# Moving operand of the 512-column weight products: stored reversed by the host, streamed with step minus one

## The reference

```python
proj = rmsnorm(x) @ w_in                  # 2048 -> 6144
x = x + mixed @ w_out                     # 2048 -> 2048
x = x + relu(rmsnorm(x) @ w_up)**2 @ w_down
proj2 = rmsnorm(x) @ w_in_2               # 2048 -> 7168
x = x + mixed2 @ w_out_2
y = (gate * gelu(xn @ u.T)) @ v           # 16384 experts
```

## Time and profile before

| what | value |
|---|---|
| device time, three runs | 3211.2 us median (3210.97 to 3211.51) |
| span of the profiled execution, first to last instruction | 3209.0 us |
| device time of the profiled execution itself | not listed; the median lies 2.2 us above the span |
| PE busy | 3191.6 us, 99% |
| PE weight loads (overlapping PE) | 2854.0 us, 89% |
| DVE, ACT, POOL busy | 2030.1, 1447.3, 496.9 us |
| DMA | 644 MB, 201 GB/s on average |
| matmul records | 19,975 |

### The profile page before, as it was taken

One profiled execution on the slowest core, in us unless ns is written; L12 is line 12 of the kernel. 1 busy time (PEld: TensorE's weight loads), 2 busy tenths in 40 slices (PEclk: granted clock), 3 DMA queues, 4 the chain that ended last, 5 costly groups with the idle time before them and its releaser, 6 DMA issues.

```text
span 3209.0 us, 48201 instructions
## 1 busy us (share of the span) xinstructions
PE 3191.6 (99%) x19975; PEld 2854.0 (89%) x19975; DVE 2030.1 (63%) x1837; ACT 1447.3 (45%) x1271; POOL 496.9 (15%) x418
## 2 busy tenths in 40 slices
PE   9999999999999999999999999999999999999999
PEld 7888899999999888888989999999999888888887
DVE  5455665556555667765476888999975555555554
ACT  5454453333433364464444444555544433334333
POOL 0000000000000002136200002888840000000000
PEclk9999999999999999999999999999999999999999
DMA  7444565555555453342255566677676656556563
GB/s 282 165 159 158 172 225 194 196 186 193 195 187 193 158 183 119 132 158 105 93 211 204 199 216 222 224 251 251 229 263 259 241 225 261 228 230 257 226 261 118
DMA packets 129572, 644.18 MB, mean 201 GB/s; under 512 B 12672, under 2 KB 45840, under 8 KB 60304
## 3 DMA queue, kind: packets, MB, share of 16 engines
q1 hardware_dynamic: 95792, 623.03, 53.3%
q10 hardware_dynamic: 33632, 18.99, 1.9%
HBM read 606.31 MB, written 35.66 MB: 200 GB/s over the span
## 4 chain that ended last, share of the span: by engine, by line
PE 97%; DVE 1%; ACT 1%; DMA 0%; SPq 0%; issue 0%; DVEq 0%; ACTq 0%
PE pj L305 12%; PE pj L304 12%; PE pj L306 12%; PE pj L282 7%; PE pj L281 7%; PE pj L280 7%; PE pj L1774 4%; PE pj L1772 4%; PE pj L890 4%; PE pj L892 4%; PE pj L1773 4%; PE pj L891 4%; PE pm L282 2%; PE pt L282 2%; PE pt L281 2%; PE pm L281 2%
## 5 line engine op out<-in xcount | busy, mean ns | idle before, releaser
L262 ACT ACTIVATE hi<-raw 128x2048 fp32r<-128x2048 f32 x534 | 1023.8, 1917 | 1372.7 <-PE pj L306 640.7
L269 DVE TENSOR_TENSOR lo<-raw,hi 128x2048 fp32r<-128x2048 f32 x400 | 918.5, 2296 | 677.5 <-ACT hi L262 676.7
L304 PE MATMUL pj<-xh,hi 128*128 128x256 f32 x3328 | 919.9, 276 | 0.0
L305 PE MATMUL pj<-xl,hi 128*128 128x256 f32 x3328 | 918.8, 276 | 0.0
L306 PE MATMUL pj<-xh,lo 128*128 128x256 f32 x3328 | 918.8, 276 | 0.0
L305 PEld LDWEIGHTS pj<-xl,hi 128*128 128x128 f32 x3328 | 625.0, 188 | 0.6
L304 PEld LDWEIGHTS pj<-xh,hi 128*128 128x128 f32 x3328 | 624.8, 188 | 0.6
L306 PEld LDWEIGHTS pj<-xh,lo 128*128 128x128 f32 x3328 | 624.8, 188 | 0.0
L269 DVE TENSOR_TENSOR lo_in<-raw,hi 128x2048 fp32r<-128x2048 f32 x134 | 308.1, 2300 | 268.9 <-ACT hi L262 268.4
L2495 POOL TENSOR_SCALAR hotA<-cst,slotT 128x128 fp32r<-128x128 f32 x256 | 337.9, 1335 | 462.0 <-ACT slotT L2333 425.4
L1772 PE MATMUL pj<-hi,xh 128*128 128x512 f32 x576 | 232.3, 403 | 0.0
(11 more groups left out here) (408 smaller groups left out, 4243.8 us busy)
## 6 DMA issues: line engine op xcount, KB each, us to landing
raw<-w_peer SPq DMA_DIRECT2D x256, 1024.0 KB, 6.3
raw<-w_mlp SPq DMA_DIRECT2D x128, 1024.0 KB, 4.8
raw<-w_in SPq DMA_DIRECT2D x102, 1024.0 KB, 4.8
raw<-w_out SPq DMA_DIRECT2D x32, 1024.0 KB, 4.8
raw<-w_q SPq DMA_DIRECT2D x16, 1024.0 KB, 4.9
act_scratch<-hidU SPq DMA_DIRECT2D x32, 512.0 KB, 3.0
gates_scratch<-stage ACTq DMA_DIRECT2D x8, 2048.0 KB, 17.5
hidV<-act_scratch SPq DMA_DIRECT2D x32, 512.0 KB, 3.7
```

The source lines that it names most:

```text
L262: nc.scalar.activation(hi[:, j, :], raw[:, j, :], ACT.Copy).then_inc(hi_ready, 1)
L269: nc.vector.tensor_tensor(low(q)[:, j, :], raw[:, j, :], hi[:, j, :].bitcast(F32), ALU.subtract).then_inc(lo_ready, 1)
L304: nc.tensor.matmul(o, hi[:, j, cols], xh[:, k0 + k, :], start=clears, stop=False, skip_group_check=True)
L305: nc.tensor.matmul(o, hi[:, j, cols], xl[:, k0 + k, :], start=False, stop=False, skip_group_check=True)
```

## The change

Every moving operand of a column product gets a reversed view: the matmul reads the run of 512 values from its last to its first, with an access step of -1 value. So that the output columns stay in place, the host stores each run of 512 in the opposite order, with a new function `backward` applied to the chunks of the two mixers' input and output projections, of `w_down` and of `v`. The up products and their arrays (`w_up`, `w_q`, `u`) are not touched. The fifteen changed lines on the device are five times the same three:

```diff
@@ multiply (multiply_tile, parts_pe and both dense functions alike)
-                    nc.tensor.matmul(pair[:, t, :], sh[:, k0 + k, tok], hi[:, j, cols], start=begin, stop=False)
-                    nc.tensor.matmul(pair[:, t, :], sh[:, k0 + k, tok], lo[:, j, cols], start=False, stop=False)
-                    mm = nc.tensor.matmul(pair[:, t, :], sl[:, k0 + k, tok], hi[:, j, cols], start=False, stop=end)
+                    nc.tensor.matmul(pair[:, t, :], sh[:, k0 + k, tok], hi[:, j, cols][:, ::-1], start=begin, stop=False)
+                    nc.tensor.matmul(pair[:, t, :], sh[:, k0 + k, tok], lo[:, j, cols][:, ::-1], start=False, stop=False)
+                    mm = nc.tensor.matmul(pair[:, t, :], sl[:, k0 + k, tok], hi[:, j, cols][:, ::-1], start=False, stop=end)
...
+def backward(c):
+
+    return np.ascontiguousarray(c.reshape(-1, P, 4, NB)[..., ::-1]).reshape(-1, P, CH)
...
-        "w_in": up_chunks(w_in[:, :W1]).reshape(G1, 4, P, CH)[list(IN1_ORDER)].reshape(4 * G1, P, CH),
-        "w_out": half_chunks(up_chunks(f(w_out)[0])),
-        "w_mlp": ffn_chunks(up_chunks(f(w_up)[0]), down_chunks(f(w_down)[0])),
-        "w_in2": up_chunks(w_in_2[:, :W2]).reshape(G2, 4, P, CH)[list(IN2_ORDER)].reshape(4 * G2, P, CH),
-        "w_out2": half_chunks(up_chunks(f(w_out_2)[0])),
+        "w_in": backward(up_chunks(w_in[:, :W1])).reshape(G1, 4, P, CH)[list(IN1_ORDER)].reshape(4 * G1, P, CH),
+        "w_out": backward(half_chunks(up_chunks(f(w_out)[0]))),
+        "w_mlp": ffn_chunks(up_chunks(f(w_up)[0]), backward(down_chunks(f(w_down)[0]))),
+        "w_in2": backward(up_chunks(w_in_2[:, :W2])).reshape(G2, 4, P, CH)[list(IN2_ORDER)].reshape(4 * G2, P, CH),
+        "w_out2": backward(half_chunks(up_chunks(f(w_out_2)[0]))),
...
-                             np.ascontiguousarray(v).reshape(4 * PEER_SB, P, CH)),
+                             backward(np.ascontiguousarray(v).reshape(4 * PEER_SB, P, CH))),
```

More of the change, by code:

```diff
@@ L289, in multiply_tile @@
                 cols = slice(k * NB, (k + 1) * NB)
-                nc.tensor.matmul(pair[:, t, :], sh[:, k, tok], hi[:, j, cols], start=False, stop=False)
-                nc.tensor.matmul(pair[:, t, :], sh[:, k, tok], lo[:, j, cols], start=False, stop=False)
-                mm = nc.tensor.matmul(pair[:, t, :], sl[:, k, tok], hi[:, j, cols], start=False, stop=end and k == 3)
+                nc.tensor.matmul(pair[:, t, :], sh[:, k, tok], hi[:, j, cols][:, ::-1], start=False, stop=False)
+                nc.tensor.matmul(pair[:, t, :], sh[:, k, tok], lo[:, j, cols][:, ::-1], start=False, stop=False)
+                mm = nc.tensor.matmul(pair[:, t, :], sl[:, k, tok], hi[:, j, cols][:, ::-1], start=False, stop=end and k == 3)
             return mm
@@ L578, in parts_pe @@
                         tok = slice(t * P, (t + 1) * P)
-                        nc.tensor.matmul(pair[:, t, :], xh[:, 4 * j + k, tok], hi[:, j, cols], start=j == 0 and k == 0, stop=False)
-                        nc.tensor.matmul(pair[:, t, :], xh[:, 4 * j + k, tok], lo_in[:, j, cols], start=False, stop=False)
-                        mm = nc.tensor.matmul(pair[:, t, :], xl[:, 4 * j + k, tok], hi[:, j, cols], start=False, stop=False)
+                        nc.tensor.matmul(pair[:, t, :], xh[:, 4 * j + k, tok], hi[:, j, cols][:, ::-1], start=j == 0 and k == 0, stop=False)
+                        nc.tensor.matmul(pair[:, t, :], xh[:, 4 * j + k, tok], lo_in[:, j, cols][:, ::-1], start=False, stop=False)
+                        mm = nc.tensor.matmul(pair[:, t, :], xl[:, 4 * j + k, tok], hi[:, j, cols][:, ::-1], start=False, stop=False)
             mm.then_inc(pe_used, 1)
@@ L889, in dense @@
                         begin, end = first and kk == 0, last and kk == 3
-                        nc.tensor.matmul(pair[:, t, :], xh[:, k0 + kk, tok], hi[:, j, cols], start=begin, stop=False)
-                        nc.tensor.matmul(pair[:, t, :], xh[:, k0 + kk, tok], lo_in[:, j, cols], start=False, stop=False)
-                        mm = nc.tensor.matmul(pair[:, t, :], xl[:, k0 + kk, tok], hi[:, j, cols], start=False, stop=end)
+                        nc.tensor.matmul(pair[:, t, :], xh[:, k0 + kk, tok], hi[:, j, cols][:, ::-1], start=begin, stop=False)
+                        nc.tensor.matmul(pair[:, t, :], xh[:, k0 + kk, tok], lo_in[:, j, cols][:, ::-1], start=False, stop=False)
+                        mm = nc.tensor.matmul(pair[:, t, :], xl[:, k0 + kk, tok], hi[:, j, cols][:, ::-1], start=False, stop=end)
                         if kk == 3 and t == 0 and last:
```

## The result

The changed kernel takes 3274.64 us (median of four runs, 3274.41 to 3274.75), the kernel before 3211.2; the ratio is 1.0198, with a 95% interval of 1.0183 to 1.0212. The profiled execution has a span of 3272.7 us, 63.7 more than before.

What follows compares the result with a forecast made beforehand. PE, busy 3191.6 of 3209.0 us, was taken to bound the kernel. The sum was 7,872 products x d, with d = 0, on the median of 3211.2 us: forecast 3211.2 us, range 3,089 to 3,333.

Steps and rivals of the forecast that it cites:

- The bound and the count: Whole kernel: PE has no slack, so any slowdown is paid in full; the change touches 7,872 products at 228.8 ns.
- The first products' 0.43 us: Kernel start: first products begin 0.43 us apart, read as the clock's lower level, 512 columns at 1.2 GHz (427 ns).
- term d: Touched 512-column products: change in pace of one product, taken as 0, with bounds of -15.5 and +201 ns.
- small-fee rival: Moving-operand reads: upward fetch-ahead loses a little per line or start, 15.5 ns a product, 122 us, 3,333 us; chance 0.12.
- lost fast stream: TensorE's moving-operand reading: fast stream needs step +1; otherwise +201 ns a product, 1,582 us, 4,793 us; chance 0.11.
- cost of nothing for the untouched products: Up products (lines 304 to 306) and attention matmuls: they stay as they are, cost 0.
- same: Touched products: pace unchanged, d = 0 or within 0.8 ns of it, time 3211.2 us; chance 0.68.
- likeliest case: Whole kernel: d = 0, no change, 3211.2 us; alone it would lie within 3,205 to 3,218 us; chance 0.68.

## Why the prediction was wrong

**The bound and the count held.** PE paid every nanosecond: 13.57 us for 3,072 reversed v products alone, 4.4 ns each, with no cover from any engine. The 7,872 products and the paces read from the earlier trace rows were the right units. The first products' 0.43 us were rightly read as the lower level of the clock: the clock record kept in the trace starts only at 12.0 us, at the full level, just where the steps shrink to 0.23 us, and the line in the earlier trace rows shows as full what has no record before that.

**The step that failed first is the term d.** It was put at 0 because "the array consumes the same elements from the same 2 KB at the same addresses". It measured 4.44 ns a product, 34.9 us by the count. The reason missed that the order in which groups of 16 bytes are asked for matters, not only which they are: reversed groups cost the whole 4.44 ns, reversal within the groups nothing. Why the order matters is open. The small-fee rival had the right kind and sign, and its bound of 15.5 ns held it; what it took for the mechanism, a loss at each line or start, is out by the runs above. The argument against it, that "the 512-column pace hardly varies (228.8 to 229.0)", does not hold in the kernel before. From 53.1 us on, 24 forward products of the first projection follow each other at 233.3 ns. Their records are longer, too; the ones of line 890 from 53.6 to 58.4 us have a mean of 398 ns, where v has 388:

```profile
L890 PE MATMUL pj<-hi,xh 128*128 128x512 f32 x7 | 2.8, 398 | 0.0
```

The bound of +201 ns for a lost fast stream was of the right size, but belongs to another change: a step of +2 has about that, +224 ns.

**The step that failed second is the cost of nothing for the untouched products.** The text said of the up products that they "stay as they are", and that a difference in the 256-column stretches "would mean that the cause is not the moving operand". They differed, by 31.3 us, and this half was not in the sum at all. The sign itself was misread: the moving operand is a cause all the same, and the 256-column stretches differ through the pace in which it left TensorE. Where the pace changes, the order of time of the changed kernel shows, at the head of the query stage:

```profile
1694.91 0.28 PE L306 MATMUL pj<-xh,lo 128*128 128x256 f32 x1
...
1700.02 0.28 PE L306 MATMUL pj<-xh,lo 128*128 128x256 f32 x1
1700.13 1.03 PE L495 MATMUL pm<-cst,resid 128*128 128x128 f32 x8
...
1701.24 0.28 PE L306 MATMUL pj<-xh,lo 128*128 128x256 f32 x1
...
1701.95 0.28 PE L306 MATMUL pj<-xh,lo 128*128 128x256 f32 x1
```

The first pair is 45 products apart: 5.11 / 45 = 113.6 ns, the fast pace, behind the reversed products of block 2's last projection and a set of transposes. Then come eight more float32 transposes, of line 495, and behind them 0.71 / 6 = 118 ns, which stays. The kernel before has the same transposes in the same place, and there they switch the other way:

```profile
1676.24 0.28 PE L306 MATMUL pj<-xh,lo 128*128 128x256 f32 x1
...
1681.55 0.28 PE L306 MATMUL pj<-xh,lo 128*128 128x256 f32 x1
1681.66 1.04 PE L495 MATMUL pm<-cst,resid 128*128 128x128 f32 x8
```

5.31 / 45 = 118.0 ns in front of them. A record's mean duration tells the two paces apart, too (281 and 276 ns). From 1676.2 to 1681.4 us, in front of the transposes,

```profile
L305 PE MATMUL pj<-xl,hi 128*128 128x256 f32 x15 | 4.2, 281 | 0.0
```

and from 1683 to 1709 us, behind them:

```profile
L305 PE MATMUL pj<-xl,hi 128*128 128x256 f32 x77 | 21.3, 276 | 0.0
```

So the changed kernel entered the query stage at the other pace than the kernel before, and eight transposes which stand in both turned fast to slow in the one and slow to fast in the other. The reversal's part in this half is indirect, through the state that it left. With the mixers reversed the u stage came out slow as well, with only v reversed it did not. The same pair stands at the head of the feed-forward layer (48 products at one pace, eight transposes, then the other pace), and it repeats: all five traces with reversed projections go from fast to slow at both places, and all thirteen with everything in front of v read forward go from slow to fast. Why a switch goes one way and not the other is open.

**What was in the trace already.** The slow entry just shown, from 1676.2 to 1681.7 us, stands in the kernel before. A mean or a median over the 3,328 products of a line (276 ns both) hides the 16 slow ones of that stretch. The pace taken stretch by stretch would have shown two values and raised the question of what picks one; then "same" at 0.68 would have been too much.

**The forecast of the range.** The measured 3274.64 us lies within 3,089 to 3,333, through the small-fee rival, while the likeliest case had no change. That it lies there is luck in part: by the reversed products alone it would be some 3,246 us, and the other half comes from an effect that no rival named.

## What to carry to other kernels

Read a moving operand upward in memory, and with neighbours adjacent: in this kernel a fully downward order cost 4.4 ns a product at 256 and at 512 columns, and a step of two doubled the time. Where TensorE is the bound, read its pace stretch by stretch and not as a mean: here the same code ran at 113.3 or 117.8 ns a product by what stood in front of it. A changed pace in code that was not touched is then a state to look for, and a few products of another shape in front of the stretch can test it cheaply (here 0.7 us that gave back 26.9).

## What the runs showed of the hardware that was not expected

- Two settled paces of forward float32r products at full granted clock, 113.3 and 117.8 ns at 256 columns, 228.9 and 233.3 at 512, each kept for hundreds of microseconds; a few other products in front can switch them, and in these traces the same work in front always gave the same pace.
- The fast pace at 512 columns is a cycle of three steps, 226, 229 and 232 ns; at the slower one all steps are alike.
- Read in descending groups of 16 bytes, only the slower pace; groups of 32 bytes the same on average; groups of 64 bytes 237.7 ns; groups of 256 bytes no loss.
- Steps of +2 and +4: 453 and 461 ns for 512 columns, about twice the forward pace and nearly equal to each other.
